# Reordering the first block of a two-block transformer kernel: w_out's high parts, keys, gated rows and squares

## The reference, cut to what matters

```python
def first_block(x, ...):                      # x: 256 tokens x 1024
    hn = rmsnorm(x, attn_norm_g)
    q, k, v, u, vg = split(hn @ w_in)         # 1024 x 2560
    sb_out = stick_breaking_attention(q, k, v)        # 8 heads of 64
    sg_out = chunked_spatial_gating(u, vg, ...)       # 8 groups of 64
    mixed = concat([rmsnorm(sb_out, g_sb), rmsnorm(sg_out, g_sg)])
    h = x + mixed @ w_out                     # 1024 x 1024
    h = h + hierarchical_moe(rmsnorm(h), ...) # 32 experts, 2 of 8 in 1 of 4 groups
    return rmsnorm(h, final_norm_g)

def stick_breaking_attention(q, k, v):        # A[t,s] for s < t only
    z = q @ k.T / 8
    log_1m_beta = where(mask, log_sigmoid(-z), 0)
    after = reverse_cumsum(log_1m_beta) - log_1m_beta
    a = where(mask, exp(log_sigmoid(z) + after), 0)
    return a @ v
```

## Time and profile before

| | us |
|---|---|
| median of 3 runs | 1056.74 |
| lowest and highest | 1056.04, 1059.1 |
| the profiled execution, its time | 1057.94 |
| its span on the core | 1056.2 |
| PE busy | 882.2 (84%) |
| PEld busy | 710.0 (67%) |
| DVE busy | 524.4 (50%) |
| ACT busy | 350.6 (33%) |
| POOL busy | 114.5 (11%) |

### The profile page before, as it was taken

How to read it: one execution, slowest core, us unless ns; L and a number is a source line. 1 busy time by engine, 2 the same in 40 slices (tenths; PEclk the granted TensorE clock), 3 DMA queues, 4 the chain that set the end, 5 groups by cost and what they waited for, 6 DMA issues and landing times.

```text
span 1056.2 us, 18017 instructions
## 1 busy us (share of the span) xinstructions
PE 882.2 (84%) x7861; PEld 710.0 (67%) x7861; DVE 524.4 (50%) x848; ACT 350.6 (33%) x471; POOL 114.5 (11%) x54
## 2 busy tenths in 40 slices
PE   8998989883764647574757899999999999999997
PEld 8997856441432324242423699599999999988985
DVE  4557563231120313121121699999997766544542
ACT  5646210100000000000001654477667454523521
POOL 1004000000000000000010587506010000000000
PEclk9999999887787878787888999999999999999999
DMA  9845499999999999999999555245477644455421
GB/s 343 261 159 239 192 377 427 428 425 427 429 428 428 429 429 428 429 429 428 428 429 404 170 197 166 76 143 176 160 245 245 221 166 161 160 188 209 161 80 40
DMA packets 86624, 299.99 MB, mean 284 GB/s; under 512 B 12265, under 2 KB 50597, under 8 KB 74149
## 3 DMA queue, kind: packets, MB, share of 16 engines
q1 hardware_dynamic: 86421, 299.13, 72.4%
q10 hardware_dynamic: 144, 0.00, 0.0%
HBM read 298.07 MB, written 1.05 MB: 283 GB/s over the span
## 4 chain that ended last, share of the span: by engine, by line
PE 50%; DMA 31%; DVE 14%; ACT 2%; issue 2%; SPq 1%; POOL 1%; DVEq 0%; ACTq 0%; POOLq 0%
DMA mem<-in_w_up 25%; PE PS L1899 11%; PE PS L1900 11%; PE PS L1901 11%; PE PS L2133 8%; DVE PS L1652 6%; PE PS L2146 3%; DMA mem<-in_w_down 3%; DMA mem<-in_w 2%; DVE ring_rest L1627 2%; DMA mem<-in_w_in 1%; PE PS L2119 1%; DVE mem L1715 1%; ACT mlp_hi L1098 1%; PE PS L1873 1%
## 5 line engine op out<-in xcount | busy, mean ns | idle before, releaser
L2133 PE MATMUL PS<-mem 128*32 128x256 f32 x2048 | 159.0, 478 | 134.4 <-DMA mem<-in_w_up 133.8
L2133 PEld LDWEIGHTS PS<-mem 128*32 128x32 f32 x2048 | 82.8, 137 | 212.3 <-issue 146.1
L1901 PE MATMUL PS<-HT_hi,ring_rest 128*128 128x256 f32 x752 | 213.2, 284 | 0.0
L1901 PEld LDWEIGHTS PS<-HT_hi,ring_rest 128*128 128x128 f32 x752 | 144.4, 192 | 0.0
L1427 DVE TENSOR_TENSOR mem<-mem,PS 128x128 f32<-128x128 f32 x32 | 12.1, 379 | 261.5 <-ACT mem L876 261.5
L1899 PE MATMUL PS<-HT_hi,z_hi 128*128 128x256 f32 x432 | 122.5, 284 | 1.1 <-ACT mem L986 1.1
L1900 PE MATMUL PS<-HT_rest,z_hi 128*128 128x256 f32 x432 | 122.2, 283 | 0.0
L1790 DVE TENSOR_TENSOR ring_rest<-mem,mlp_hi 128x4096 fp32r<-128x4096 f32 x16 | 70.8, 4424 | 59.3 <-ACT mlp_hi L1098 59.2
L876 ACT ACTIVATE mem<-PS 128x128 f32<-128x128 f32 x32 | 8.9, 277 | 272.7 <-PE PS L2133 272.7
L692 POOL TENSOR_TENSOR ring_rest<-mem,z_hi 128x2048 fp32r<-128x2048 f32 x19 | 87.6, 4626 | 88.4 <-DVE mem L1702 46.7
L1652 DVE SCALAR_TENSOR_TENSOR PS<-mem,CAW,PS 128x256 f32<-128x256 f32 x232 | 91.3, 485 | 0.0
(11 more groups left out here) (351 smaller groups left out, 1768.7 us busy)
## 6 DMA issues: line engine op xcount, KB each, us to landing
mem<-in_w_up SPq DMA_DIRECT2D x32, 2048.0 KB, 20.9
...
```

What stands on the lines that cost most here:

```text
L1901: ins = nc.tensor.matmul(dst, s_rest, m_hi, start=False, stop=stop and n == len(terms) - 1, skip_group_check=True)
L2133: ins = nc.tensor.matmul(PS[SLOTS * j:SLOTS * (j + 1), bank, 0:2 * F_STRIP].rearrange("p (w n) -> p w n", w=2), xg[:, k, :], w[:, :, k, F_ ...
```

## The change

In the first block and nowhere else the order of work is written anew:

- The high parts of w_out's halves 0 and 1 are made right behind a table load on ScalarE, ahead of `split_in1(9)`, and lie in slot 2 instead of slot 4. The halves are made in the order 0, 1, 2, 3 instead of 2, 3, 0, 1.
- GpSimd makes the rests of halves 0, 1 and 2, VectorE only that of half 3 (before: GpSimd 2 and 0, VectorE 3 and 1).
- w_up of expert 1 is loaded behind `out1_ps` 14, as slot 2 is taken until then; w_gate of expert 0 is loaded behind expert 2's weights, as slot 4 is free.
- `take_qk(7)` stands inside `att_softplus(2)`, between its first pass and the mask.
- On TensorE `qk_chunk(3)` stands ahead of the wait for the tables, the gated products 0 and 1 come first, `weighted_values(3)` stands between gated products 2 and 3, and the products of attention pairs 0 to 2 follow in one row. The gated rows' gains, high parts and rests come earlier on VectorE and ScalarE.
- The squares of the attention's four pairs are added on GpSimd (three additions of 128x256), and TensorE sums over partitions once instead of four times (L2085).

```diff
@@ -225,7 +225,7 @@
...
         out1_hi = [parts(f"out1_hi{n}", mem_at + 4 * at, KC, HALF)
-                   for n, at in enumerate((4 * SLOT_FLOATS, 4 * SLOT_FLOATS + HALF_FLOATS, 3 * SLOT_FLOATS, 3 * SLOT_FLOATS + HALF_FLOATS))]
+                   for n, at in enumerate((2 * SLOT_FLOATS, 2 * SLOT_FLOATS + HALF_FLOATS, 3 * SLOT_FLOATS, 3 * SLOT_FLOATS + HALF_FLOATS))]
@@ -426,7 +426,6 @@
...
-        OUT1_SPLIT = (2, 3, 0, 1)
@@ -546,18 +545,18 @@
...
-            sp.wait_ge(*in1_used(5))
-            load_part(wu_d, 1, *first[1])
...
             load_down(THIRD_EXPERT, *third[2])
+            load_part(wg_d, 0, *second[0])
...
             sp.wait_ge(out1_ps, 14)
-            load_gate_up(0, second)
+            load_part(wu_d, 0, *second[1])
+            load_part(wu_d, 1, *first[1])
@@ -679,13 +678,20 @@
...
-            for n in OUT1_SPLIT[0::2]:
+            for n in range(3):
                 raw, rest = out1_half(n)
-                pool.wait_ge(out1_hi_ready, OUT1_SPLIT.index(n) + 1)
+                pool.wait_ge(out1_hi_ready, n + 1)
...
                 ins.then_inc(out1_rest_pool, 1)
+
+            for pair in range(1, PAIRS):
+                pool.wait_ge(sq_ready, pair + 1)
+                ins = nc.gpsimd.tensor_tensor(att_sq[:, 0, :], att_sq[:, 0, :], att_sq[:, pair, :], ALU.add)
+                if pair < PAIRS - 1:
+                    link(ins)
+            ins.then_inc(sum_ready, 1)
@@ -810,7 +816,7 @@
...
                 if n % 2 == 0:
-                    act.wait_ge(*in1_used(8 if n == 2 else IN1_HALVES - 1))
+                    act.wait_ge(*in1_used((5, 8)[n // 2]))
@@ -821,6 +827,8 @@
...
             act.preload_act_table_set("natural_log_exp_and_others")
+            split_out1(0)
+            split_out1(1)
@@ -838,24 +846,22 @@
...
                 add_squares(so[:, tt, :], 6 + tt, square[:, 0:SB])
-            split_out1(OUT1_SPLIT[0])
+            split_out1(2)
...
             att_weights(1)
-            split_out1(OUT1_SPLIT[1])
-            split_out1(OUT1_SPLIT[2])
+            split_out1(3)
+            split_hT("mix", range(TT))
             att_log(3)
-            split_hT("mix", range(TT))
-            att_weights(2)
...
             split_att(1)
-            split_out1(OUT1_SPLIT[3])
+            att_weights(2)
...
             act.wait_ge(scale_ps, 2)
-            nc.scalar.activation(rstd[:, 4:4 + TT], PS[:, 0, 0:TT], ACT.Sqrt, scale=1.0 / SB, bias=eps[:, :]).then_inc(rms_ready, 1)
+            nc.scalar.activation(rstd[:, 4:4 + TT], PS[:, 2, 0:TT], ACT.Sqrt, scale=1.0 / SB, bias=eps[:, :]).then_inc(rms_ready, 1)
@@ -1225,11 +1231,13 @@
...
-            def att_softplus(pair):
+            def att_softplus(pair, between=()):
...
                 link(nc.vector.scalar_tensor_tensor(t, score_banks(pair), 0.0, t, ALU.max, ALU.add))
+                for m in between:
+                    take_qk(m)
@@ -1254,7 +1262,7 @@
...
                 raw, rest = out1_half(n)
-                dve.wait_ge(out1_hi_ready, OUT1_SPLIT.index(n) + 1)
+                dve.wait_ge(out1_hi_ready, n + 1)
@@ -1268,7 +1276,7 @@
...
             def add_gated(half, tt):
-                dve.wait_ge(out1_ps, 4 * (1 - half) + tt + 3)
+                dve.wait_ge(out1_ps, 4 * half + tt + 3)
@@ -1289,28 +1297,26 @@
...
             att_masked(1)
-            att_softplus(2)
-            take_qk(7)
+            att_softplus(2, (7,))
             apply_gain("mix", G_MIX, range(TT))
-            rest_out1(OUT1_SPLIT[1])
-            att_masked(2)
-            rest_hT("mix", range(TT))
...
             gain_att(1)
-            att_softplus(3)
+            rest_hT("mix", range(TT))
+            att_masked(2)
...
             rest_att(1)
-            rest_out1(OUT1_SPLIT[3])
+            att_softplus(3)
+            rest_out1(3)
+            att_masked(3)
             gain_att(2)
-            att_masked(3)
...
             for tt in range(TT):
-                add_gated(1, tt)
+                add_gated(0, tt)
...
             for tt in range(TT):
-                add_gated(0, tt)
+                add_gated(1, tt)
@@ -2020,12 +2026,8 @@
...
-            def out1_rest_made(n):
-                order = OUT1_SPLIT.index(n)
-                pe.wait_ge(out1_rest_dve if order % 2 else out1_rest_pool, order // 2 + 1)
-
             def gated_product(n):
-                out1_rest_made(n)
+                pe.wait_ge(*((out1_rest_pool, n + 1) if n < 3 else (out1_rest_dve, 1)))
@@ -2040,9 +2042,9 @@
...
             turn_tables()
+            qk_chunk(3)
...
             scores(0)
-            qk_chunk(3)
@@ -2058,32 +2060,23 @@
...
             later_keys(2)
+            gated_product(0)
+            gated_product(1)
+            later_keys(3)
+            weighted_values(2)
...
             gated_product(2)
+            weighted_values(3)
             gated_product(3)
-            later_keys(3)
-            weighted_values(2)
-            gated_product(0)
-            gated_product(1)
+            pe.wait_ge(x_ready, 2)
             pe.wait_ge(att_x, 4)
-            pe.wait_ge(hT_rest_ready, split_count("mix", TT + 1))
-            for n in (2, 3):
-                for tt in range(TT):
-                    out1_product(n, tt, slice(0, 2))
-            weighted_values(3)
             pe.wait_ge(hT_rest_ready, split_count("mix", TT + 2))
-            for n in (2, 3):
-                for tt in range(TT):
-                    out1_product(n, tt, slice(2, 3))
-            pe.wait_ge(x_ready, 4)
-            for n in (0, 1):
+            for n in range(4):
...
                     out1_product(n, tt, slice(0, 3))
-            pe.wait_ge(sq_ready, PAIRS)
+            pe.wait_ge(sum_ready, 1)
             for tt in range(TT):
-                for pair in range(PAIRS):
-                    ins = nc.tensor.matmul(PS[:, 0, tt:tt + 1], att_sq[:, pair, tt * P:(tt + 1) * P], ones[:, 0:1],
-                                           start=pair == 0, stop=pair == PAIRS - 1, skip_group_check=True)
+                ins = nc.tensor.matmul(PS[:, 2, tt:tt + 1], att_sq[:, 0, tt * P:(tt + 1) * P], ones[:, 0:1], start=True, stop=True)
@@ -2357,12 +2350,12 @@
...
             z_round(IN2_HALVES // IN2_GROUP - 1, True)
-            pe.wait_ge(sum_ready, 1)
+            pe.wait_ge(sum_ready, 2)
...
                 if n == 4:
-                    pe.wait_ge(sum_ready, 2)
+                    pe.wait_ge(sum_ready, 3)
```

## The result

The changed kernel takes 1047.78 us (median of 4 runs, 1047.33 to 1049.18) beside 1056.39 us of the kernel before on the same chip: a ratio of 0.991, with a 95% interval of 0.9893 to 0.9927. On another chip, later, the same pair gave 1047.82 us (6 runs) beside 1057.27 us (11 runs), 0.9911, 0.9894 to 0.9928. (The first ratio isn't the quotient of its two medians, which is 0.992.) Put against the 1056.74 us on which the prediction was made, 0.991 means 1047.2 us; put against its own series' 1056.39 us it means 1046.9 us. The profiled execution took 1048.01 us, with a span of 1046.3 us, where the one before had 1057.94 and 1056.2 us. So the change brings 9.5 us by the ratio, where 8.0 were forecast: right in direction and mechanism, too small in size, with the result at the very bottom of the range (1047.0 us), on it or just outside it.

The account below looks back on a forecast made before the run. TensorE's run through the w_out product was taken to set when the expert weight stream starts. Losses of 8.8 us removed less a new 0.9 us, about 8.0 with smaller gaps, took 1056.74 to 1048.7 us; range 1047.0 to 1052.8 us.

Parts of the forecast that it names:

- near 116 us: Turning of X on TensorE, at the end of the w_out product: forecast there, where the profile had 124.05 us.
- The four waits: TensorE idle ahead of first scores 0.97, last scores 1.50, first gated product 2.45, w_out's first block 1.20 us: losses to remove.
- the clock's 1.4 us: Behind the wait ahead of the first gated product: some 15 matmuls at the 1.2 GHz level, 1.4 us to save.
- The squares: Sixteen one-column matmuls on TensorE, 1.84 us, shrink to a quarter: 1.3 us taken as saved.
- GpSimd's early halves: Two early w_out rests on GpSimd, 5.1 us each, from about 52.5 to 63 us, wanted at 88 us: nothing on the path.
- 9.5 us of free time: VectorE from 50 to 76 us: busy 16.48 of 26 us, the rest free for at most 6.4 us of waiting for GpSimd.
- 2.45 us become 0.9 us: Ahead of the first gated product: HT_rest at 88.4 us, TensorE there at 87.45 us, so a new wait of 0.9 us.
- the fewer changes between kinds of products: Small gaps on TensorE: they bring the w_out product's gain from 7.9 to about 8.0 us.
- no new wait, 0.7 us of small gaps gone: Lower bound of the forecast's own case, which alone spans 1047.2 to 1050.5 us: 1047.2 us.
- The third wait staying: Rival: VectorE still last at the first gated product, clock falls, only 5.0 us go: 1051.7 us, chance 0.21.
- The waits did not come back further on: Rival: margins at pair 3's exponential and add_gated(0) missed by about 2.5 us each, 3 us remain: 1053.7 us, chance 0.11.
- The slow clock: Rival: TensorE's clock at 0.50 through gated and w_out products, up to 17.5 us: 1066.2 us, chance 0.04.

Follow-up runs that it names:

- d_fill: Changed kernel with five useless 512-column matmuls on TensorE ahead of w_out's last eight low-part products: 1051.93 us (4 runs).
- u_early: Changed kernel without the early high parts of w_out's halves 0 and 1, so GpSimd makes its remainders later: 1051.23 us (6 runs).
- u_gated: Changed kernel with VectorE's old order: half 3's rest and pair 2's masks ahead of HT_rest, attention gains behind it: 1051.50 us (1 run).

## Why the prediction was right in kind and short in size

**The bound.** Right. The stream of weights starts when TensorE frees the slots: the DMA share ahead of expert 3's load is 0.12 as before, and d_fill shows the passage to that load one for one. "Near 138 us" for that load was 137.52; "near 116 us" for the turning of X was 115.31.

**The four waits.** 0.97, 1.50, 2.45 and 1.20 us: all removed, as in the sum, but for a new one of 0.39 us in the third's place, and the clock's 1.4 us with the third. The times given on the way were met: mask products of pair 2 to 85.3 us (85.5 forecast), first gated product at 88.05 (88.4).

**The squares.** 1.3 us forecast, 1.34 measured. An addition on GpSimd takes 0.74 us (0.6 and at most 1.3 forecast) and the last ends at 104.0 us, 8 us ahead of TensorE:

```profile
103.27 0.74 POOL L691 TENSOR_TENSOR mem<-mem 128x256 f32<-128x256 f32 x1 [4.35 <-ACT mem L826]
```

**GpSimd's early halves.** Two at 5.1 us were to end at 63 us; they took 14.3 and ended at 67.0 us, since a piece takes 1.8 us beside VectorE's passes and not 1.27. It cost nothing, as the prediction's 9.5 us of free time said. But the early place was costed as if it brought nothing of its own, and u_early shows 2.5 us: with GpSimd quiet from 84.7 us on (79.67 and 5.04 us of its last remainder), VectorE's two subtractions for HT_rest take 1.28 us there and not 2.70.

**The step that failed** is a size in the sum and not the mechanism: the term of the new wait, "2.45 us become 0.9 us". It was 0.39. The steps of VectorE ahead of it were rounded up a little (the masks end at 85.33 us and not 85.5, the gains take 1.20 us and not 1.27, the attention's gains are done at 87.31 us and not 87.7; only the subtraction itself was as forecast), so that HT_rest was put at 88.4 us and came 0.35 us sooner, and TensorE, put there at 87.45 us, came at 87.66, 0.2 us later. 0.5 us of the missing size is here. The other 0.3 us are the second mis-sized term, the 0.1 us for "the fewer changes between kinds of products": B is 8.83 us shorter and the new wait 0.39, so 9.2 us of losses went, where 8.8 were summed, and these gaps were worth 0.4 us. They have no rows of idle time, and no run takes them apart. So the w_out product ends 8.8 us sooner, not 8.0. Both misses lie inside the prediction's own bounds for this case (no new wait, 0.7 us of small gaps gone: 1047.2 us).

**The rest of the gap is outside the sum.** The end came 9.9 us earlier in the profiles. Of this 1.15 us arise behind expert 3's load, in work that the change doesn't touch. The largest piece lies between 863.9 and 957.6 us, which the changed kernel passes in 1.6 us less: behind an idle time of TensorE that both kernels have, the profile of the kernel before has a fall of the clock that the changed one lacks (windows of both, the kernel before first; the changed kernel is there 8.6 us sooner):

```profile
876.00:880.00 4.00, 2.84 (x14) 2.87 (x15) 3.25 (x2) 1.83 (x5) 0.00 (x0) 0.67 0.82 282
```

```profile
867.00:871.00 4.00, 2.46 (x21) 2.50 (x22) 3.30 (x4) 2.21 (x5) 0.00 (x0) 1.00 0.70 240
```

In the table above the rest varies from 906.8 to 910.4 us at the same volume of loads. So I take this piece for chance of the execution: there is one trace of the kernel before, and no run tests it. The range's lower edge, 1047.0 us, lay 1.7 us below the forecast and took in the step's own uncertainty (no new wait, smaller gaps) and next to nothing for this; the result came out 1.5 to 1.8 us below the forecast by the ratio (1047.2 or 1046.9 us). That end wanted another microsecond or two.

**The rivals.** The third wait staying is what u_gated shows (3.9 of the 8.8 us at the turning of X lost, which leaves 4.9, where the rival said 5.0). Its condition didn't hold because the 3.25 us went from between the gains and HT_rest. The waits did not come back further on: the exponential of pair 3 starts at 97.93 us and ends at 98.8, 0.8 us ahead of its reader at 99.58 (0.5 forecast), and add_gated(0) ends at 102.0 us, 1.4 us ahead (0.9 forecast). The slow clock stayed away: the granted clock is 1.00 up to the turning of X.

**What the prediction didn't see** is that in the kernel before a second wait, for the masks, lay hidden behind the third. The forecast came out because the changed order has both answers in it; someone who had taken the reordering on VectorE alone for "2.45 us and the clock" would have forecast 3.9 us of gain and found 3 us of loss.
